# The gated delta rule in chunks of 64 on quarters of TensorE's array, with projection and scan in one block

## The reference

```python
GDN_HEADS = 8
GDN_DK = 64
GDN_DV = 64
CONV_W = 4
GDN_CHUNK = 64
...
def _gdn(qkv, a, b, z, conv_buf, s0, conv_w, conv_b, a_log, dt_bias, gnorm):
    u, conv_new = _short_conv(qkv, conv_buf, conv_w, conv_b)
    q, k, v = jnp.split(u, [GDN_QK_WIDTH, 2 * GDN_QK_WIDTH], axis=-1)
    q = _l2norm(q.reshape(B, T, GDN_HEADS, GDN_DK))
    k = _l2norm(k.reshape(B, T, GDN_HEADS, GDN_DK))
    beta = jax.nn.sigmoid(b.astype(jnp.float32))
    g = -jnp.exp(a_log) * jax.nn.softplus(a.astype(jnp.float32) + dt_bias)
    o, s_new = _gated_delta(q, k, v, g, beta, s0)
    o = _rmsnorm(o, gnorm).reshape(B, T, GDN_WIDTH) * jax.nn.silu(z)
...
# in _gated_delta, for each chunk of C tokens and each head
    gc = jnp.cumsum(ch3(g), axis=-1)
    decay = jnp.exp(jnp.where(tri, gc[..., :, None] - gc[..., None, :], -jnp.inf))
    kb = kc * bc[..., None]
    lmat = jnp.where(strict, jnp.einsum('...id,...jd->...ij', kb, kc) * decay, 0.0)
    tmat = lax.linalg.triangular_solve(eye + lmat, eye, left_side=True, lower=True)
    u = tmat @ (vc * bc[..., None])
    w = tmat @ (kb * jnp.exp(gc)[..., None])
    a_intra = jnp.where(tri, jnp.einsum('...id,...jd->...ij', qc, kc) * decay, 0.0)
    def step(s, xs):
        v_new = u_ - w_ @ s
        o = (q_ * jnp.exp(g_)[..., None]) @ s + a_ @ v_new
        s = s * jnp.exp(g_last)[..., None] + jnp.einsum('bhcd,bhce->bhde', k_ * jnp.exp(g_last - g_)[..., None], v_new)
```

## Time and profile before

| quantity | value |
| --- | --- |
| device time, median of 3 runs (range) | 2068.03 us (2067.95 to 2068.67) |
| time of the profiled execution | 2074.15 us |
| its span, first to last instruction | 2072.5 us |
| mean granted TensorE clock | 0.951 |
| stage_gdn_project, from its first product to its last transpose | 844.3 to 1112.2 us |
| set-up of stage_gdn_scan, to the first product of an inverse | 1112.2 to 1144.3 us |
| the eight prompt tiles | 1144.3 to 1511.1 us |
| sample tile and end of the block | 1511.1 to 1573.3 us |
| stage_output | 1573.3 to 2072.5 us |

### The profile page before, as it was taken

One profiled execution on the slowest core, in us unless ns is written; L12 is line 12 of the kernel. 1 busy time (PEld: TensorE's weight loads), 2 busy tenths in 40 slices (PEclk: granted clock), 3 DMA queues, 4 the chain that ended last, 5 costly groups with the idle time before them and its releaser, 6 DMA issues. The chain is left out here.

```text
span 2072.5 us, 27449 instructions
## 1 busy us (share of the span) xinstructions
PE 1853.7 (89%) x9974; PEld 1304.1 (63%) x9974; DVE 840.4 (41%) x1707; ACT 457.9 (22%) x1056; POOL 114.4 (6%) x222
## 2 busy tenths in 40 slices
PE   3899997899999967899994999999967999999998
PEld 2555567677777744566663888888834666666443
DVE  3210012887777742014454666555576100100133
ACT  2000002555555530101223222222201000000011
POOL 0000000000000012000002111111100000000000
PEclk9899998999999977999996999999987999999999
DMA  8203202130000023101103000000002300100021
GB/s 344 100 0 113 91 3 70 46 137 21 1 0 1 0 76 106 65 21 40 41 0 37 1 1 0 0 0 0 1 3 82 142 31 31 61 31 0 21 81 46
DMA packets 57807, 95.65 MB, mean 46 GB/s; under 512 B 17747, under 2 KB 45948, under 8 KB 53564
## 3 DMA queue, kind: packets, MB, share of 16 engines
q1 hardware_dynamic: 54060, 84.93, 12.1%
q10 hardware_dynamic: 2352, 5.38, 0.7%
q0 software_dynamic: 1312, 4.20, 0.6%
HBM read 86.09 MB, written 12.55 MB: 48 GB/s over the span
## 5 line engine op out<-in xcount | busy, mean ns | idle before, releaser
L165 PE MATMUL ogP<-hT,ow 128*128 128x352 f32 x768 | 232.9, 464 | 10.2 <-DMA oo<-in_w_o 10.2
L165 PE MATMUL gfP<-hT,gw 128*128 128x352 f32 x768 | 229.2, 461 | 7.1 <-DMA gw<-in_w_feat 7.1
L165 PEld LDWEIGHTS ogP<-hT,ow 128*128 128x128 f32 x768 | 147.4, 192 | 94.3 <-DMA oo<-in_w_o 11.8
L165 PEld LDWEIGHTS gfP<-hT,gw 128*128 128x128 f32 x768 | 146.5, 191 | 88.6 <-DMA gw<-in_w_feat 7.3
L800 PE MATMUL poP<-kvt,ppT 128*128 128x128 f32 x1056 | 156.7, 283 | 18.5 <-ACT ppT L858 12.1
L800 PEld LDWEIGHTS poP<-kvt,ppT 128*128 128x128 f32 x1056 | 133.7, 193 | 32.0 <-issue 11.5
L773 PE MATMUL sP<-zbT,qb 128*128 128x512 f32 (+3 forms) x384 | 142.3, 481 | 5.6 <-DVE ss L884 2.9
L165 PE MATMUL featP<-hT,w 128*128 128x352 f32 x384 | 115.8, 464 | 4.9 <-DMA w<-in_w_feat 4.9
L841 ACT ACTIVATE ss<-ss,nm 128x640 f32<-128x640 f32 (+7 forms) x128 | 94.0, 735 | 83.3 <-DVE nm L891 83.3
L1369 PE MATMUL psA<-x,lt 128*128 128x128 f32 (+1 forms) x784 | 98.8, 279 | 15.2 <-ACT xt L1482 13.3
L225 PE MATMUL tokP<-cmp_in,hT 128*128 128x404 f32 (+1 forms) x288 | 100.9, 514 | 8.6 <-PEq L66 8.6
(11 more groups left out here) (336 smaller groups left out, 2422.2 us busy)
## 6 DMA issues: line engine op xcount, KB each, us to landing
cmp_in<-in_w_ada SPq DMA_DIRECT2D x5, 2048.0 KB, 13.7
cmp_in<-in_cmp_pool SPq DMA_DIRECT2D x56, 128.0 KB, 2.1
gw<-in_w_feat SPq DMA_DIRECT2D x7, 1024.0 KB, 4.8
ow<-in_w_gm SPq DMA_DIRECT2D x7, 1024.0 KB, 4.9
hT<-in_xT SPq DMA_DIRECT2D x8, 528.0 KB, 7.0
w<-in_w_feat SPq DMA_DIRECT2D x4, 1024.0 KB, 6.4
qkv<-in_w_out SPq DMA_DIRECT2D x2, 2048.0 KB, 11.5
qkv<-in_x SPq DMA_DIRECT2D x8, 512.0 KB, 3.2
```

Source lines behind the costliest of these rows:

```text
L165: mm = pe.matmul(out[:, b, 0:TB], w[:, k, ft * P:(ft + 1) * P], x[:, k, b * TB:(b + 1) * TB], start=(k == 0), stop=(k == KT - 1))
```

## The change

The two blocks of the delta rule become one, stage_gdn. What it does:

- The features run in the order u0 to u4, s0, u5 to u8, s1, u9 to u11, z0 to z3, where u are the groups of k, q and v, z the gate's, and s0 and s1 are sums of squares as 12 thin products on PE (line 1188). The norms enter as logarithms: ACT takes Ln of the sums, and decay, beta and norm are added as logarithms along the tokens before one Exp. q, k and v stay feature-major (uT); nothing is turned to token-major form ahead of the scan.
- 23 steps (step, placed by E_AT) stand between the products of the feature groups: sums of logarithms, their spread over the rows, and the key and query products in 64 x 64 blocks, whose results become the matrices LT and AT for all tiles.
- The inverse works on chunks of 64, two chunks of a tile at once, in 5 levels. Every product is 64 x 64 on one quarter of the array, four side by side (indices HALF in the code). The transposes remain on the whole array, a half (a) at a time.
- The state runs over 16 chunks of 64. A chunk's chain has three parts, A (products with S), B (with the inverse) and C (update and output). The six parts of the two chunks of tile t - 1 stand in the levels of tile t, at the slots of CHAIN_AT; the turning of keys and values (turn_tokens) at slot 13. The chains of the last tile stand alone at the end.
- The sample tokens' work is cut in ten pieces (sample), which stand in the levels of tile 0.
- The weights come in halves of 512 KB with three buffers. The loop over tiles is written out. stage_output reads the result from where the new stage leaves it, and its last weight in two halves.

```diff
-def stage_gdn_project(nc, T):
...
-def stage_gdn_scan(nc, T):
...
-                                mm = pe.matmul(A[0:m, product_bank(li, a), h % 4 * P:h % 4 * P + m], lt[0:m, h, 0:m], x[0:m, h, 0:m])
...
-                                l_, r_ = (xt, yy) if li < nl - 1 else (yy, xt)
-                                mm = pe.matmul(Bk[0:m, a, h % 4 * P:h % 4 * P + m], l_[0:m, h, 0:m], r_[0:m, h, 0:m])
...
+def stage_gdn(nc, T):
...
+        ORDER = [("u", 0), ("u", 1), ("u", 2), ("u", 3), ("u", 4), ("s", 0), ("u", 5), ("u", 6), ("u", 7), ("u", 8), ("s", 1),
+                 ("u", 9), ("u", 10), ("u", 11), ("z", 0), ("z", 1), ("z", 2), ("z", 3)]
+        E_AT = {("u", 1, 3): 0, ("u", 2, 3): 1, ("u", 3, 3): 2, ("u", 4, 3): 3, ("u", 10, 5): 4}
+        for n_, at_ in enumerate([("u", 11, 5), ("u", 11, 6), ("u", 11, 7), ("z", 0, 0), ("z", 0, 5), ("z", 0, 7), ("z", 1, 0), ("z", 1, 1), ("z", 1, 2), ("z", 1, 4),
+                                  ("z", 1, 5), ("z", 1, 6), ("z", 1, 7), ("z", 2, 0), ("z", 2, 1), ("z", 2, 2), ("z", 2, 3), ("z", 2, 4)]):
+            E_AT[at_] = 5 + n_
+        CHAIN_AT = {1: ("A", 0), 3: ("B", 0), 5: ("C", 0), 7: ("A", 1), 9: ("B", 1), 11: ("C", 1)}
...
+                        if k == KT - 1:
+                            mm.then_inc(prod, 1)
+                        if (kind, i, k) in E_AT:
+                            step(E_AT[kind, i, k])
+                def square_sums(pos, i):
+                    pe.wait_ge(sq_ready, 4 * (i + 1))
+                    for b in range(3):
+                        for j in range(NJ):
+                            mm = pe.matmul(fP[pos % 2][Q32[j], b, 0:TB], ind[:], zbT[:, j, b * TB:(b + 1) * TB])
+                    mm.then_inc(s_prod, 1)
...
+                    elif e < 19:
+                        a, p = (e - 15) // 2, (e - 15) % 2
+                        for t in range(QT):
+                            for h2, c in quads:
+                                k_ = tok(4 + 2 * a + p, 2 * t + c)[HALF[h2]]
+                                mm = pe.matmul(eP[HALF[c], h2, t * HD:(t + 1) * HD], k_, k_)
...
+                def turn_inverse(t, i, a):
+                    for h2 in range(2):
+                        mm = pe.transpose(ps[:, 4 + a, h2 * P:(h2 + 1) * P], x[:, a, h2].rearrange("p q t -> p (q t)"), ident[:])
+                    mm.then_inc(tr[a], 1)
...
+                def system_product(t, li, a):
+                    pe.wait_ge(xs[a], 6 * t + li + 1)
+                    for h2 in range(2):
+                        for c, p in quads:
+                            mm = pe.matmul(ps[HALF[p], 2 * a + c, h2 * HD:(h2 + 1) * HD], LT[HALF[c], t, slot(a, h2, p), :], x[HALF[c], a, h2, p, :])
+                    mm.then_inc(p1[a], 1)
...
+                def inverse_product(t, li, a):
+                    pe.wait_ge(xtr[a], 6 * t + li + 1)
+                    pe.wait_ge(yr[a], NL * t + li + 1)
+                    for h2 in range(2):
+                        for p, c in quads:
+                            mm = pe.matmul(ps[HALF[c], 2 * a + p, h2 * HD:(h2 + 1) * HD], xt[t % 2][HALF[p], a, h2, c, :], yy[HALF[p], a, h2, c, :])
+                    mm.then_inc(p2[a], 1)
...
+                def chain(n, what):
+                    t, c = n // 2, n % 2
+                    if what == "A":
+                        if n:
+                            pe.wait_ge(cS, n)
+                            pe.wait_ge(cO, n)
...
+                        for k, at_ in ((4, 0), (0, 128)):
+                            for a in range(2):
+                                for h2, p in quads:
+                                    mm = pe.matmul(ps[HALF[p], 6 + h2, at_ + a * HD:at_ + (a + 1) * HD], tok(k + 2 * a + p, n)[HALF[h2]], S[HALF[h2], 2 * a + p, :])
+                        mm.then_inc(cA, 1)
+                    elif what == "B":
+                        pe.wait_ge(cQ, n + 1)
+                        for a in range(2):
+                            pe.wait_ge(xtr[a], 6 * t + 6)
...
+                                mm = pe.matmul(ps[HALF[a], 6 + p, 256 + h2 * HD:256 + (h2 + 1) * HD], xt[t % 2][HALF[p], a, h2, c, :], r[HALF[p], 2 * a + h2, :])
+                        mm.then_inc(cB, 1)
+                    else:
+                        pe.wait_ge(cV, n + 1)
+                        pe.wait_ge(vk_ready, 2 * t + 2)
+                        for p in range(2):
+                            for a, h2 in quads:
+                                pe.matmul(ps[HALF[h2], 6 + a, p * HD:(p + 1) * HD], kr[HALF[a], c, 2 * p + h2, :], vz[HALF[a], 2 * p + h2, :])
+                        for h2 in range(2):
+                            for a, p in quads:
+                                mm = pe.matmul(ps[HALF[p], 6 + a, 384 + h2 * HD:384 + (h2 + 1) * HD], AT[HALF[a], 2 * p + h2, n, :], vz[HALF[a], 2 * p + h2, :])
+                        mm.then_inc(cC, 1)
...
+                def between(t, s):
+                    if t == 0 and s < 10:
+                        sample(s)
+                    if t and s in CHAIN_AT:
+                        what, c = CHAIN_AT[s]
+                        chain(2 * (t - 1) + c, what)
+                    if s == TURN_AT:
+                        turn_tokens(t)
+                for t in range(QT):
+                    for a in range(2):
+                        turn_inverse(t, 0, a)
+                    between(t, 0)
+                    for li in range(NL):
+                        for a in range(2):
+                            system_product(t, li, a)
+                        between(t, 3 * li + 1)
+                        for a in range(2):
+                            inverse_product(t, li, a)
+                        between(t, 3 * li + 2)
+                        for a in range(2):
+                            turn_inverse(t, li + 1, a)
+                        between(t, 3 * li + 3)
+                for c in range(2):
+                    for what in "ABC":
+                        chain(2 * (QT - 1) + c, what)
...
+                        act.wait_ge(u_ready, f + 1)
+                        act.activation(zbT[:, f % 4, SMP], us, ACT.Square)
+                        act.activation(chunks(zbT[:, f % 4, 0:SEQ]), u, ACT.Square).then_inc(sq_ready, 1)
...
+                        dve.transpose(x[:, a].rearrange("p h q t -> p (h q t)"), xi[:, 256 * a:256 * (a + 1)]).then_inc(xs[a], 1)
...
+def by_heads(v, p):
+    return v.rearrange("p (a q h) -> p a q h", a=2, q=2)[:, :, p, :].unsqueeze(3)
```

More of the change, by code:

```diff
@@ L1063, in silu @@
+                act.wait_ge(g_step, 3)
+                act.activation(ga[:, 1], ga[:, 1], ACT.Ln).then_inc(e_act, 1)
                 def silu(f):
+                    u, us = prompt(CONV[f]), late(CONV[f])
                     act.wait_ge(conv_ready, f + 1)
[L1065 to L1071 removed]
@@ L1079, in _ @@
+                n_u = {f: pos for pos, (kind, f) in enumerate(ORDER) if kind == "u"}
+                for f in range(12):
+                    act.wait_ge(prod, f + 1)
                     if f >= 2:
@@ new lines, in between @@
+                def between(t, s):
+                    if t and s in CHAIN_AT and CHAIN_AT[s][0] == "B":
+                        new_values(2 * (t - 1) + CHAIN_AT[s][1])
+                    if s == TURN_AT:
+                        for i, buf in enumerate((vb, kr)):
+                            act.wait_ge(turned, 2 * t + i + 1)
+                            if t:
+                                act.wait_ge((cR, cC)[i], 2 * t)
+                            else:
+                                act.wait_ge(s_pe, 10)
+                            act.activation(buf.rearrange("p c u e -> p (c u e)"), ps[:, 4 + i, :], ACT.Copy).then_inc(tcopy, 1)
@@ new lines, in new_values @@
+                def new_values(n):
+                    act.wait_ge(cB, n + 1)
+                    if n:
+                        act.wait_ge(cC, n)
+                    else:
+                        act.wait_ge(s_pe, 10)
+                    act.activation(vz.rearrange("p (q h) e -> p q h e", q=2), ps[:, 6:8, 256:256 + 2 * HD].rearrange("p q (h e) -> p q h e", h=2), ACT.Copy).then_inc(cV, 1)
+                for t in range(QT):
+                    for a in range(2):
+                        copy_turned(t, 0, a)
+                    between(t, 0)
+                    for li in range(NL):
+                        between(t, 3 * li + 1)
+                        between(t, 3 * li + 2)
+                        for a in range(2):
+                            copy_turned(t, li + 1, a)
+                        between(t, 3 * li + 3)
@@ new lines, in _ @@
+                for f in range(12):
+                    if f == 11:
+                        system_decays()
+                    convolve(f)
+                    if f < 4:
+                        read_step(f)
+                    if f == 4:
+                        sums(0)
+                    if f == 6:
+                        rows_of_k()
+                    if f == 8:
+                        sums(1)
```

(4 more changed lines are left out.)

1210 lines of the change are left out of this document (622 added, 588 removed).

## The result

The changed kernel takes 1820.93 us in the median (1819.92 to 1821.76, 4 runs), the kernel before 2068.31: a ratio of 0.8796, 95% interval 0.8783 to 0.8808, 247 us less. The prediction was 1855 with a range of 1828 to 1918. Its direction was right; its saving was some 34 us too small, and the time lies 7 us under the range.

A forecast was written before the change was run, and what follows sets the result against it. PE was taken as the limit (busy 89%). Projection 297, tile 0 41, six tiles 140, tile 7 and last chunks 34.7, block's end 3.5: 516.2 against 729.0, 212.8 us saved, giving 1855, range 1828 to 1918.

The forecast's parts named there:

- the price of a quarter product: Scan and projection steps: a 64-column record on one quarter costs 29.5 ns instead of 118, read from stage_compress.
- The 3.80 predicted for C: Scan level with chain part C, whose 32 records stand ahead of the transposes: 3.80 us in all.
- The level with A and B: Scan level with chain parts A and B and three DVE operations ahead of the subtractions: 5.34 us.
- the second mis-sized term: DVE operations on 256 elements in the scan's levels: 0.42 us each, the next waiting the full time.
- Tile 0: First scan tile, with sample pieces and no chain: 41 us, bounds -9 and +15, including 17.3 for 288 thin records.
- The projection: Features, 23 steps, mode changes, sums of squares, waits and clock loss: 297 us, no gain against 300.0 with set-up before.
- The three waits: Projection: PE idle 4.3 us ahead of s0, the same at s1, 3.2 in z0; together 11.9, plus 5.7 clock loss.
- Mode changes: Tile-size switches on PE: 0.09 us per change, without the full drain that would add about 10 us in the whole.
- Evacuation: Rival in the scan: DVE's PSUM reads become the limit, about +41 us, 1896; chance 0.18 together with slow hand-offs.
- The clock fell: Rival in the scan: PE's waits lower the granted clock, +110 us, 1965; chance 0.10. The forecast expected above 0.95.
- Quarters do not take turns: Rival: quarters' weights load one after another, a record costs 118 ns, kernel 2230 us; chance 0.05 with like collapses.
- Better than 1828: Case below the range: waits at s0 and s1 covered and thin records cheap at once; chance 0.05.

The follow-up runs named there:

- wide run: Changed kernel with the inverse's level products streaming 128 columns instead of 64, same number of instructions: ratio 0.8811 to the kernel before.
- the wide level products: 128-column level products together with preparing the next tile's x later on POOL, in the changed kernel: ratio 0.8818 to the kernel before, 0.8764 without the wide products.
- the later x: Changed kernel with POOL's preparation of the next tile's x issued behind the second chain's subtraction: ratio 0.8764 to the kernel before, 6.6 us less.
- three moves of instructions: Changed kernel with next tile's x, the sums of squares and the steps from the tenth on all placed later: 1796.21 us, ratio 0.8672 to the kernel before.
- the doubled run: Changed kernel with every quarter product of the scan issued twice into the same place: ratio 0.9227 to the kernel before, 89 us more.
- the batches measured alone: Changed kernel plus batches of 32 products that nothing uses, behind the last feature group: 15 ns a record in the scan's order; no kernel time given.

## Why the prediction was wrong

**The step that failed is the price of a quarter product**: "a record of 64 columns costs 29.5 ns". The nearest row by form and size had an operand read at every 16th token; without that a record costs 15 ns. The prediction's bounds for it pointed upward only (10 ns more, 118 as the other end); below 29.5 it allowed nothing, and the range ended at 1828, above the measured 1820.93. The other row of the same group, 54.8 ns for 256 columns, pointed to it: 64 columns at that rate are 13.7.

**What follows from it, level by level.** With 28 ns for the level products and 15 in the chain, the wide run's undisturbed levels are 3.34 with C and 5.05 for the last (1256.75 to 1261.80 would be the prediction's 5.04). The 3.80 predicted for C, less 32 records at 14.3 ns, is 3.34: the working held, its price did not. The level with A and B was predicted at 5.34; less 48 records at 14.3 it is 4.65, and 4.22 was measured in that run (1208.09 to 1212.31). Some 0.3 of the 0.43 left are five DVE operations that start 0.34 after one another and not 0.42, the second mis-sized term (1.87 us in the wide run, 1250.83 to 1252.70, where the prediction allowed 2.18); the last 0.1 stays open. Undisturbed, the changed kernel's levels are 3.81, 2.83, 3.81, 2.83 and 4.43, 17.7 us a tile instead of 23.3. Of these 5.6 us the wide level products brought back 2.6 (20.3 us a tile), and 11 of the kernel's 34. The other 3 are worked out and not run: 160 chain records at 14.3 ns are 2.3, DVE's spacing in two levels 0.6.

**What was missed on the other side.** The six tiles take 19.9 and not 17.7. A part of the difference is POOL holding up line 1759 and the lower clock behind the wait, 7.8 us in six tiles as the later x showed. The prediction left out that POOL's operations could lengthen DVE's. The rest, some 5 us, goes with gaps marked issue and lower clock; it was not taken apart. Tile 0 came near (37.7 against 41) by errors that cancel: its quarter batches were cheaper, and its 288 thin records took some 13.7 us of PE, 0.047 each, instead of 17.3, but its granted clock was 0.64, which the prediction had not priced there.

**Terms that held.** The projection: 297.1 against 297, but by errors that cancel. Steps and mode changes took 39.8 instead of 47.2 (the quarter price again: the eight key and query steps 8.7 instead of 15.1), sums of squares 6.1 instead of 3.6 (lower clock), features 239 instead of 234.5 with cold start and clock loss. The three waits were right in place; the sum is luck in part (0.7 less than predicted for each of the first two, 1.5 more for the third). Moving them gave back 18.9 us, where the prediction put 11.9 and 5.7 of clock on them. The clock behind them cost 5.5, near the 5.7, though the wait of stage_output from which this price was read cost nothing in the changed kernel's trace. Mode changes: in the wide run the transposes start at 1256.16, four in 0.66 us, and the next quarter batch at 1256.75. That is 0.2 us after the last transpose's start (1256.82 - 0.28 = 1256.54), less than the 0.28 of a full drain: the prediction's reading held.

**The rivals.** Evacuation did not happen (DVE at 65% in the six tiles, 256 elements in 0.42). The clock fell only in part (0.93 in the six tiles, under the 0.95 that was forecast). Quarters do not take turns. "Better than 1828" came true by another way than the one named: the waits at s0 and s1 were not covered.

## What to carry to other kernels

A price taken from another product should agree in how its operands are read, not only in form and size, and a second row at another width tells whether it does. Bound a unit price on both sides before it is multiplied by some thousands. Where two engines are given work side by side, look for operations with both inputs in SBUF on DVE beside POOL's reads, and for work queued behind a wait on PE: here three moves of instructions, none of them less work, were worth 25.7 us.

## What the hardware showed unexpectedly

Records of 64 columns on four quarters follow each other at 15 ns, and thin ones of 8 columns as well; 128 x 128 records take 113. A stride of 16 tokens in the moving operand doubles the 15 ns. Two products running on one quarter cost next to nothing (16 ns), four do (37). Behind the same wait of 3.20 us in the same code the clock fell in some executions and not in others. Where PE takes a record every 31 ns (186.18 us for 5954 records in six tiles of the doubled run), there are gaps of up to 1.8 us without a releaser; at 40 ns (121.82 us for 3074) hardly any are left, 0.8 us in the whole scan. In the batches measured alone, too, a gap of 0.79 us follows 167 records at 15 ns. What makes these gaps was not tested.
